# First normalization by token halves with renumbered weight slots, and another VectorE order in the feed-forward units

## The chip, the cores and the metric

One core of a Trainium2 chip runs the whole program. The metric is the device time of one execution in microseconds, lower is better. TensorE multiplies, VectorE, ScalarE and GpSimd work on tiles, and transfers go through queues, most of them SyncE's.

## What is computed

The reference is one layer for 512 tokens of width 1024 in float32: an adaptive modulation, a pooling branch and a recurrent branch mixed by gates, then

```python
mixed = (g_pool * y_pool + g_rwkv * y_rwkv) @ w_out[l]
x = layer_norm(ALPHA * x + (1 + gt1) * mixed, ln1_g[l], ln1_b[l], LN_EPS).astype(x.dtype)
h = x * (1 + sc2) + sh2
f = jnp.square(jax.nn.relu(h @ w_ff1[l])) @ w_ff2[l]
x = layer_norm(ALPHA * x + (1 + gt2) * f, ln2_g[l], ln2_b[l], LN_EPS).astype(x.dtype)
```

`w_out` is 1024x1024, `w_ff1` 1024x4096, `w_ff2` 4096x1024. The change concerns these five lines alone.

## The kernel before

**Split products.** Every float32 operand is split into a high part (ScalarE, `split_hi`, L762, or `split_again`, L1114) and a low part, raw minus high (GpSimd L669, L725 and L732, or VectorE `low_tile`, L1515). A product is three matmuls: high by high, low by high, high by low. Weights come in tiles of 128x1024 in order k; each tile has a slot of `w_hi` and `w_lo`, and its high part waits until TensorE is done with the tile that had the slot before.

**Output product** (L2184). The weights `w_out` are eight pairs o of 24 matmuls each. o=0 to 3 give columns 0 to 511, o=4 to 7 columns 512 to 1023, in four PSUM banks, one for each row block of 128 tokens. `take_out` (L1594, L1567) adds a bank to `xrows` and takes its statistics; `spreads` (L1574, L1575) and `columns` (L1580, L1581) make mean, variance and factors for two row blocks, ScalarE's `root` (L1067) the root between them.

**First normalization.** ScalarE normalizes row blocks 0 to 2 (L1072), VectorE block 3 (L1627). TensorE turns eight 128-column blocks f (L2191) into banks 4 to 7, 512 tokens each. For each f VectorE modulates (`h2_f32`, L1632), ScalarE makes the high part (L1081) and the residual `res` (L1082), and the low part is VectorE's for even f (L1635) and GpSimd's for odd f (L720). TensorE multiplies chunks 0 and 1 of `w_ff1` with each f as it comes (L2221), then chunks 2 and 3 (L2232). The high parts of the weights of chunks 2 and 3 stand in ScalarE's order behind its last residual, their low parts in GpSimd's order behind its last odd f. Chunks 0 and 1 use the slots of pairs o=6 and o=7.

**Units.** The feed-forward part runs in eight units of four chunks; units 1 to 6 are a hardware loop, unit 7 is written out. In a unit TensorE multiplies chunks 0 to 3 (48 + 24 + 24 matmuls of 512 columns), and ScalarE takes relu (L1089) and square (L1092) of each. The second product is a Winograd-like scheme: seven products of half-size blocks (`PRODUCTS`, 24 matmuls of 256 columns each, L2146) instead of eight. VectorE makes the sums of activations (`a_sums`, L1482 to L1486), their low parts (`low_raw` L1495, `low_sums` L1504), the sums of weights T1, T3, T2, T4 (L1528 to L1535), and adds each half product to `res` (`take`, L1563, two instructions). Product number at needs low part 4+at of the weights; those of numbers 3 to 6 are GpSimd's, in that order. A product waits until the one that had its PSUM banks before is taken: number 2 for number 0, 4 for 2, 5 for 3, 6 for 4. The second product needs `low_raw` of chunk 3 from its fourth matmul on. VectorE's order around chunk 3 is: low part of weight tile 6, T4, `lows` of chunk 3 (all three sums, `low_raw`, `low_sums`), then the fourteen takes.

**Tail.** In unit 7 TensorE turns `res` back in four steps (`turn_back`, L2124, order `BACK`), ScalarE copies the turned blocks to `xt2` (L1139), and VectorE takes statistics (L1688), makes the factors and applies them (`affine`, L1693, L1696) for row blocks 1, 2 and 3; ScalarE and GpSimd (L736, L737) do block 0. Each block is stored as it gets ready.

Of the kernel before, what the change touches and what calls it, by code (L numbers as in the profile page):

```python
# [6 lines left out]
P = 128  # L7
ALU = mybir.AluOpType
# [6 lines left out]
def build(nc, x, c, w_ada, b_ada, w_in, mu_shift, pool_mix, pool_scale, w_pool_up, w0, w_decay_up, a0,  # L15
# [6 lines left out]
    KT = D // P  # L22
# [23 lines left out]
    with ctx:  # L46
# [286 lines left out]
        SLOT = (2, 0, 1, 3, 2, 0, 1, 3, 2, 0, 1)  # L333
# [170 lines left out]
        BACK = ((0, 0, 2), (1, 1, 0), (0, 1, 2), (1, 0, 6))  # L504
# [30 lines left out]
        def _(sp):  # L535
# [79 lines left out]
        def _(pool):  # L615
# [101 lines left out]
            for f in range(1, KT, 2):  # L717
                pool.wait_ge(sem("h2_f32"), f + 1)
                pool.wait_ge(sem("h2_hi"), f + 1)
                link(pool.tensor_tensor(h2_lo[:, f, :], h2_f32(f), h2_hi[:, f, :].bitcast(F32), ALU.subtract), "h2_lo_by_pool")  # L720
# [19 lines left out]
        def _(act):  # L740
# [301 lines left out]
            for n in range(1, KT):  # L1042
# [14 lines left out]
                mixed_hi(n)  # L1057
            link(act.activation(small[:, 56:57], ones_col[:, :], ACT.Sqrt))
# [5 lines left out]
            def root(g, stage):  # L1064

                act.wait_ge(sem("ln_eps"), 2 * stage + g + 1)
                link(act.activation(small[:, 32 + 2 * g:34 + 2 * g], small[:, 28 + 2 * g:30 + 2 * g], ACT.Sqrt), "ln_std")  # L1067
# [5 lines left out]

            root(0, 0)
            normalise(0)
            normalise(1)
            root(1, 0)
            normalise(2)
            for f in range(KT):
                act.wait_ge(sem("h2_f32"), f + 1)  # L1080
                link(act.activation(h2_hi[:, f, :], h2_f32(f), ACT.Copy), "h2_hi")  # L1081
                link(act.activation(res[:, f, :], bank[4 + f % 4], ACT.Identity, scale=small[:, f:f + 1], bias=small[:, 8 + f:9 + f]), "res_ready")  # L1082
# [58 lines left out]
            for at in range(3):  # L1141
                out_tokens(at)
# [3 lines left out]
            out_tokens(3)  # L1146
# [3 lines left out]
        def _(dve):  # L1150
# [326 lines left out]
            def a_sums(link, n):  # L1477
# [5 lines left out]
                else:  # L1483
                    link(dve.tensor_tensor(a_sum[:, 1, :], x1, right(n)[:, S // 2:S], ALU.add))
                    link(dve.tensor_tensor(a_sum[:, 2, :], a_sum[:, 1, :], x0, ALU.subtract))
                    link(dve.tensor_tensor(a_sum[:, 3, :], right(n)[:, 0:S // 2], a_sum[:, 2, :], ALU.subtract), "a_summed")  # L1486
# [61 lines left out]
            def wait_half(unit, at, row, units=0):  # L1548
# [744 lines left out]
```

## Time and profile before

| | |
|---|---|
| Three runs | 1074.05, 1074.97 (median) and 1080.8 us |
| Profiled execution | 1072.6 us, span 1070.6 us |
| TensorE, VectorE, ScalarE, GpSimd busy | 91%, 64%, 44%, 34% of the span |
| One addition or statistics of 512 columns on VectorE | 0.69 us each |
| One aggregate on VectorE | 0.22 us |
| Normalization of 128 tokens on ScalarE | 1.25 us |
| Six passes of the unit loop | 738.1 to 999.1 us, 43.5 us each |

Times in the rows are microseconds from the start of the span. A timeline line gives start, duration (of all instructions of the line, if there are several), engine, line of the kernel, operation, output<-inputs, shapes and count; in brackets the engine's idle time before it and who ended it. In a line of the chain of waits stand start, length, engine, output, line and count.

### The profile page before, as it was taken

The page shows a single profiled execution, that of the slowest core. Times are in us where ns is not written, and L with a number is a line of the kernel's source. Part 1 is how long each engine was busy: PE and PEld are TensorE (multiplying, and loading weights), DVE is VectorE, ACT ScalarE, POOL GpSimd, SP SyncE. Part 2 cuts the span into 40 slices and gives each one's busy share as a digit, 9 for nine tenths or more (in the row PEclk, how much of TensorE's full clock was granted, in tenths as well). Part 3 has the DMA queues.
Part 4 walks back from the last instruction along what each step waited for, and adds up shares of the span by engine and source line. Part 5 has one row for each costly group of instructions (what it writes and reads, how often), then busy time and mean ns, then how long its engine had stood idle before and what let it go on. Part 6 is the DMA issues. An engine that isn't in the chain of part 4 may idle for free.

```text
span 1070.6 us, 27435 instructions
## 1 busy us (share of the span) xinstructions
PE 973.7 (91%) x11539; PEld 804.4 (75%) x11539; DVE 681.7 (64%) x940; ACT 468.9 (44%) x574; POOL 359.7 (34%) x218
## 2 busy tenths in 40 slices
PE   1798899999999999899999999699999999999993
PEld 1676677786777677577788888588889898898982
DVE  5735568578748858754221354657777777687778
ACT  0336445347335632436432251473544545445351
POOL 7332511411321132126444444235134052250431
PEclk9999999999999999999999999799999999999997
DMA  9332234224332424332543527114142251332101
GB/s 370 104 95 65 80 92 134 63 81 126 105 80 86 126 62 112 90 97 51 166 110 89 166 62 229 54 40 132 47 137 79 79 156 39 118 100 76 59 1 79
DMA packets 122918, 108.03 MB, mean 101 GB/s; under 512 B 5395, under 2 KB 104641, under 8 KB 122817
## 3 DMA queue, kind: packets, MB, share of 16 engines
q1 hardware_dynamic: 113009, 83.46, 26.1%
q10 hardware_dynamic: 9808, 23.08, 7.0%
q8 instruction: 81, 1.33, 0.5%
q14 instruction: 20, 0.16, 0.0%
HBM read 100.23 MB, written 2.10 MB: 96 GB/s over the span
## 4 chain that ended last, share of the span: by engine, by line
PE 68%; DVE 18%; ACT 5%; issue 3%; DMA 3%; POOL 2%; SPq 1%; ACTq 1%; DVEq 0%; POOLq 0%
PE bank L1787 11%; PE set L2146 10%; PE bank L2232 7%; PE set L2088 6%; PE bank L2088 5%; PE set L2232 4%; PE set L1841 4%; PE set L2184 3%; PE set L1853 2%; PE bank L2146 2%; PE set L1829 2%; PE bank L1768 2%; DVE Q L1234 1%; DVE w_lo L1515 1%; PE bank L2221 1%
## 5 line engine op out<-in xcount | busy, mean ns | idle before, releaser
L669 POOL TENSOR_TENSOR w_lo<-w_raw,w_hi 128x1024 fp32r<-128x1024 f32 (+2 forms) x75 | 171.0, 2280 | 380.7 <-ACT w_hi L762 380.3
L762 ACT ACTIVATE w_hi<-w_raw 128x1024 fp32r<-128x1024 f32 (+2 forms) x81 | 81.8, 1010 | 110.2 <-PE set L2088 36.1
L791 ACT ACTIVATE Q<-set 128x1024 f32<-128x1024 f32 x56 | 57.4, 1025 | 135.2 <-PE set L1841 69.0
L1787 PE MATMUL bank<-h_hi,w_hi 128*128 128x512 f32 x256 | 107.4, 419 | 3.5 <-POOL w_lo L669 3.3
L1563 DVE SCALAR_TENSOR_TENSOR res<-set,mod,res 128x256 f32<-128x256 f32 x192 | 92.9, 484 | 27.0 <-PE set L2146 19.0
L2146 PE MATMUL set<-a_hi,w_hi 128*128 128x256 f32 x384 | 108.6, 283 | 0.0
L2146 PE MATMUL set<-a_hi,w_lo 128*128 128x256 f32 x384 | 108.4, 282 | 0.0
L1114 ACT ACTIVATE w_hi<-w_raw 128x1024 fp32r<-128x1024 f32 x70 | 74.3, 1061 | 77.9 <-PE set L2146 69.9
L2146 PE MATMUL set<-a_lo,w_hi 128*128 128x256 f32 x384 | 108.3, 282 | 0.0
L1787 PE MATMUL bank<-h_hi,w_lo 128*128 128x512 f32 x256 | 102.4, 400 | 0.9 <-issue 0.9
L1787 PE MATMUL bank<-h_lo,w_hi 128*128 128x512 f32 x256 | 102.9, 402 | 0.0
L732 POOL TENSOR_TENSOR w_lo<-w_raw,w_hi 128x1024 fp32r<-128x1024 f32 x35 | 84.1, 2403 | 16.6 <-ACT w_hi L1114 13.3
L732 POOL TENSOR_TENSOR w_lo<-w_t,w_hi 128x1024 fp32r<-128x1024 f32 x7 | 16.8, 2405 | 189.0 <-ACT w_hi L1114 189.0
L2146 PEld LDWEIGHTS set<-a_lo,w_hi 128*128 128x128 f32 x384 | 73.0, 190 | 0.3
L2146 PEld LDWEIGHTS set<-a_hi,w_hi 128*128 128x128 f32 x384 | 72.9, 190 | 0.3
L2146 PEld LDWEIGHTS set<-a_hi,w_lo 128*128 128x128 f32 x384 | 72.9, 190 | 0.0
L1787 PEld LDWEIGHTS bank<-h_hi,w_hi 128*128 128x128 f32 x256 | 48.6, 190 | 20.2 <-issue 5.8
L1787 PEld LDWEIGHTS bank<-h_hi,w_lo 128*128 128x128 f32 x256 | 48.5, 189 | 11.2 <-issue 0.7
L1787 PEld LDWEIGHTS bank<-h_lo,w_hi 128*128 128x128 f32 x256 | 48.7, 190 | 9.5 <-issue 0.7
L1515 DVE TENSOR_TENSOR w_lo<-w_raw,w_hi 128x1024 fp32r<-128x1024 f32 x38 | 46.6, 1225 | 11.0 <-ACT w_hi L1114 7.5
L2232 PE MATMUL set<-h_hi,w_hi 128*128 128x512 f32 x128 | 50.6, 395 | 0.0
L2232 PE MATMUL set<-h_lo,w_hi 128*128 128x512 f32 x128 | 50.2, 392 | 0.0
(357 smaller groups left out, 2287.5 us busy)
## 6 DMA issues: line engine op xcount, KB each, us to landing
w_raw<-in_w_ff_dram SPq DMA_DIRECT2D x64, 512.0 KB, 4.0
w_raw<-in_w_in_dram SPq DMA_DIRECT2D x46, 512.0 KB, 3.9
y<-in_w_ada_dram ACTq DMA_DIRECT2D x20, 512.0 KB, 3.7
ada<-in_w_ada_dram SPq DMA_DIRECT2D x16, 512.0 KB, 9.4
Q<-in_w_ada_dram ACTq DMA_DIRECT2D x12, 512.0 KB, 4.1
w_raw<-in_w_rwkv_up_dram SPq DMA_DIRECT2D x8, 512.0 KB, 3.8
w_raw<-in_w_out_dram SPq DMA_DIRECT2D x8, 512.0 KB, 4.4
xtok<-in_x_dram SPq DMA_DIRECT2D x4, 512.0 KB, 9.6
```

The lines of the kernel that those rows point to most:

```text
L669: link(pool.tensor_tensor(part_of(k, w_lo), raw_part(k), part_of(k, w_hi).bitcast(F32), ALU.subtract), "lo_ready")
L732: again(pool.tensor_tensor(w_lo[SLOT[m]][:, :, :], raw[:, :, :], w_hi[SLOT[m]][:, :, :].bitcast(F32), ALU.subtract), "lo_ready")
L762: link(act.activation(part_of(k, w_hi), raw_part(k), ACT.Copy), "hi_ready")
L791: link(act.activation(by_half(tile), psum_flat(set_of(name)), ACT.Copy), "act_kept")
L1114: link(act.activation(w_hi[SLOT[m]][:, :, :], raw[:, :, :], ACT.Copy), "hi_ready")
L1515: link(dve.tensor_tensor(w_lo[slot][:, :, :], raw[:, :, :], w_hi[slot][:, :, :].bitcast(F32), ALU.subtract), "lo_by_dve")
L1563: link(dve.scalar_tensor_tensor(out=res[:, f, tokens], in0=product, scalar=mod[:, 40 + f:41 + f], in1=res[:, f, tokens], op0=ALU.mult, op1 ...
L1787: mm = pe.matmul(o, w, hx, start=(m == 0), stop=(m == 3 * KT - 1))
L1841: mm = pe.matmul(ps[N * p:N * p + N, q, c * C:(c + 1) * C], by_pair(left, p, q, c), by_pair(right, p, q, c), start=(m == 0), stop=(m == le ...
L2088: mm = pe.matmul(o, w[slot_of(k)][:, kt, :], hx[:, kt, :], start=(kt == 0 and m == 0), stop=(kt == kts - 1 and m == 2))
L2146: mm = pe.matmul(to, wx[:, i, columns], a[:, form, i, :], start=OPENS[at] and b == 0 and i == 0 and m == 0, stop=i == 1 and m == 2, skip_g ...
L2232: mm = pe.matmul(bank[m][:, :], w[slot][:, kt, :], hx[:, kt, :], start=(kt == 0 and at == 0), stop=(kt == KT - 1 and at == 2))
```

## The change

It does four things. (1) `SLOT` is renumbered: chunk 0's weights now follow pair o=5 in their slot, chunk 1's take a slot unused so far, chunks 2 and 3 follow o=6 and o=7. (2) The last two pairs of the output product run for row blocks 0 and 1 first, and the first normalization, its transposes, modulation, high and low parts, residuals and the products of chunks 0 and 1 run for tokens 0 to 255 first (g=0), then for 256 to 511 (g=1). VectorE normalizes blocks 1 and 3, ScalarE blocks 0 and 2; LN_EPS is added as the bias of ScalarE's root. ScalarE's high parts for chunks 2 and 3 still follow its last residual. (3) In every unit VectorE's order around chunk 3 is `last_lows`, with the first product's takes between and T4 behind. (4) In unit 7 the fifth and sixth product are swapped, and the tail is in another order: statistics and gains of row blocks 2 and 3 read PSUM, block 1 is finished last.

```diff
-        SLOT = (2, 0, 1, 3, 2, 0, 1, 3, 2, 0, 1)
+        SLOT = (1, 3, 2, 0, 1, 3, 2, 0, 1, 3, 2)
...
+        TURN = ((4, 4, 5, 5, 2, 2, 3, 3), (6, 6, 7, 7, 4, 4, 5, 5))
...
-        BACK = ((0, 0, 2), (1, 1, 0), (0, 1, 2), (1, 0, 6))
+        BACK = ((0, 0, 2), (0, 1, 0), (1, 1, 2), (1, 0, 6))
+        PLAIN, LAST = (0, 1, 2, 3, 4, 5, 6), (0, 1, 2, 3, 5, 4, 6)
...
-            for j in (1, 0, 2, 3):
+            for j in (0, 2, 3, 1):
...
+            for g in range(2):
+                for f in range(1, KT, 2):
+                    pool.wait_ge(sem("h2_f32"), g * KT + f + 1)
+                    pool.wait_ge(sem("h2_hi"), g * KT + f + 1)
+                    link(pool.tensor_tensor(h2_lo[:, f, side(g)], h2_f32(f)[:, side(g)], h2_hi[:, f, side(g)].bitcast(F32), ALU.subtract), "h2_lo_by_pool")
...
             root(0, 0)
             normalise(0)
-            normalise(1)
+            for f in range(2):
+                row_high(0, f)
             root(1, 0)
+            for f in range(2, 4):
+                row_high(0, f)
             normalise(2)
+            for f in range(4, KT):
+                row_high(0, f)
+            for f in range(4):
+                residual(0, f)
+            for f in range(4):
+                row_high(1, f)
+            for f in range(4, KT):
+                residual(0, f)
+            for f in range(4, KT):
+                row_high(1, f)
             for f in range(KT):
...
+                residual(1, f)
             for m in range(2, 4):
                 split_hi(K_FF + m)
...
+            def last_lows(link, n, unit, units=0):
+
+                a_sums(link, n, 0)
+                low_raw(link, n, units)
+                a_sums(link, n, 1)
+                take(link, unit, 0, 0, units)
+                low_sums(link, n, units)
+                take(link, unit, 0, 1, units)
+                summed(link, "T4", unit, units)
...
             take_out(0, 1)
             take_out(1, 1)
             spreads(0)
             take_out(2, 1)
             columns(0, 0)
+            x_hat(1)
+            modulated(0, 0)
+            modulated(0, 1)
             take_out(3, 1)
+            row_low(0, 0)
             spreads(1)
+            modulated(0, 2)
+            modulated(0, 3)
             columns(1, 0)
...
+            x_hat(3)
+            row_low(0, 2)
+            for g, f in ((0, 4), (0, 6), (1, 0), (1, 2), (1, 4), (1, 6)):
+                modulated(g, f)
+                modulated(g, f + 1)
+                row_low(g, f)
...
                 if m == 2:
                     low_tile(link, 6, 0)
-                    summed(link, "T4", 0)
...
+            for at in LAST[1:5]:
                 for row in range(2):
...
+                    last_take(at, row)
+            turned_statistics(0)
+            last_take(LAST[5], 0)
             turned_statistics(1)
...
+            last_take(LAST[5], 1)
+            spreads(0)
+            last_take(LAST[6], 0)
+            columns(0, 1)
+            last_take(LAST[6], 1)
             turned_statistics(2)
...
             turned_statistics(3)
             spreads(1)
...
+            dve.wait_ge(sem("rows_in"), 32)
+            gain(2)
+            dve.wait_ge(sem("ln_std"), 4)
+            link(dve.reciprocal(small[:, 38:40], small[:, 34:36]))
+            shift(2)
+            gain(3)
+            shift(3)
+            gain(1)
+            shift(1)
...
+            for g in range(2):
+                for o in (NOUT - 2, NOUT - 1):
...
+                    mm = out_rows(o, (2 * g, 2 * g + 1))
...
+            for g in range(2):
+                for kt in range(KT):
+                    pe.wait_ge(sem(("h2_lo_by_dve", "h2_lo_by_pool")[kt % 2]), g * (KT // 2) + kt // 2 + 1)
...
+                    if g == 0 and kt == 5:
+                        pe.wait_ge(sem("out_taken"), 2 * TB)
+                        pe.wait_ge(sem("x_hat_by_dve"), 2)
+                        pe.wait_ge(sem("x_hat"), 2)
+                        for f in range(4):
+                            turn(1, f)
+                    if g == 0 and kt == KT - 1:
+                        for f in range(4, KT):
+                            pe.wait_ge(sem("res_ready"), (2, 4)[f // 6])
+                            turn(1, f)
...
             for m in (2, 3):
+                pe.wait_ge(sem("res_ready"), (6, 8)[m - 2])
                 hidden_chunk(m, 0, 0)
```

`row_high`, `residual`, `modulated` and `row_low` are the instructions of L1081, L1082, L1632 and L1635 on 256 tokens. `gain` is the first half of `affine` (for blocks 2 and 3 two instructions that read 512 columns from PSUM), `shift` the second.

## Rows read from the trace of the kernel before

**Rows 1.** The page's chain that ended last, by engine.

```profile
PE 68%; DVE 18%; ACT 5%; issue 3%; DMA 3%; POOL 2%; SPq 1%; ACTq 1%; DVEq 0%; POOLq 0%
```

**Rows 2.** Timeline of TensorE: turn, a unit, the last matmul.

```profile
686.49 1.09 PE L2191 MATMUL set<-ident,xrows 128*128 128x128 f32 x4 [6.42 <-ACT xrows L1072]
...
724.87 0.47 PE L2146 MATMUL bank<-a_hi,w_hi 128*128 128x256 f32 x1 [2.72 <-DVE a_lo L1495]
...
900.60 0.39 PE L2146 MATMUL bank<-a_hi,w_hi 128*128 128x256 f32 x1 [1.00 <-DVE a_lo L1495]
...
1050.72 0.28 PE L2146 MATMUL set<-a_hi,w_lo 128*128 128x256 f32 x1
```

**Rows 3.** Busy time by stretch: stretch, length, engines, granted clock, DMA share, GB/s.

```profile
681.00:724.90 43.90, 33.88 (x156) 28.10 (x156) 28.75 (x42) 30.38 (x43) 12.29 (x7) 0.84 0.16 45
...
686.50:690.00 3.50, 2.65 (x12) 2.25 (x13) 1.69 (x4) 1.32 (x2) 0.00 (x0) 0.50 0.19 58
```

**Rows 4.** Chain of waits in a unit: matmuls of 512, then of 256 columns.

```profile
885.28 5.62 PE set L2232 x24
...
903.39 10.65 PE set L2146 x89
```

**Rows 5.** Timeline of VectorE: the last instruction.

```profile
1066.25 1.28 DVE L1696 SCALAR_TENSOR_TENSOR xt<-xt,small,ln_rows 128x1024 f32<-128x1024 f32 x1
```

**Rows 6.** Timeline of GpSimd: low parts before and in the turn.

```profile
653.69 2.40 POOL L669 TENSOR_TENSOR w_lo<-w_raw,w_hi 128x1024 fp32r<-128x1024 f32 x1 [3.19 <-ACT w_hi L762]
...
681.38 2.34 POOL L669 TENSOR_TENSOR w_lo<-w_raw,w_hi 128x1024 fp32r<-128x1024 f32 x1 [3.19 <-ACT w_hi L762]
```

**Rows 7.** Timeline of VectorE before and in the turn.

```profile
655.07 2.10 DVE L1543 TENSOR_TENSOR w_raw<-w_raw,gate 128x1024 f32<-128x1024 f32 x1 [3.22 <-DMA w_raw<-in_w_out_dram]
...
671.05 1.22 DVE L1528 TENSOR_TENSOR w_t<-w_raw 128x1024 f32<-128x1024 f32 x1 [8.06 <-DMA w_raw<-in_w_ff_dram]
...
681.78 1.96 DVE L1581 SCALAR_TENSOR_TENSOR small<-small 128x2 f32<-128x2 f32 x1
...
689.45 1.66 DVE L1632 TENSOR_SCALAR t<-set,mod 128x512 f32<-128x512 f32 x2 [1.56 <-PE set L2191]
```

**Rows 8.** Timeline early in the kernel: VectorE one, then two operations; GpSimd.

```profile
112.92 0.69 DVE L1309 TENSOR_TENSOR Q<-t 128x512 f32<-128x512 f32 x1
113.65 3.00 DVE L1441 TENSOR_TENSOR Q<-G 128x512 f32<-128x512 f32 x2
...
113.76 2.34 POOL L701 TENSOR_TENSOR Q<-Q,DC 128x1024 f32<-128x1024 f32 x1 [3.14 <-DVE Q L1309]
```

**Rows 9.** Timeline of ScalarE at the end of the turn.

```profile
701.88 0.63 ACT L1081 ACTIVATE h_hi<-left 128x512 fp32r<-128x512 f32 x1 [0.38 <-DVE left L1632]
702.54 0.78 ACT L1082 ACTIVATE res<-set,small 128x512 f32<-128x512 f32 x1
703.35 2.15 ACT L762 ACTIVATE w_hi<-w_raw 128x1024 fp32r<-128x1024 f32 x2
...
708.53 0.42 ACT L1011 ACTIVATE a_hi<-left 128x256 fp32r<-128x256 f32 x1
```

**Rows 10.** Timeline of VectorE around chunk 3 of a unit.

```profile
897.12 1.23 DVE L1535 TENSOR_TENSOR w_raw<-w_raw 128x1024 f32<-128x1024 f32 x1
898.38 0.43 DVE L1484 TENSOR_TENSOR a_sum<-left,right_odd 128x256 f32<-128x256 f32 x1
...
899.85 0.69 DVE L1495 TENSOR_TENSOR a_lo<-right_odd,a_hi 128x512 fp32r<-128x512 f32 x1
900.70 0.96 DVE L1504 TENSOR_TENSOR a_lo<-a_sum,a_hi 128x768 fp32r<-128x768 f32 x1 [0.15 <-ACT a_hi L1022]
...
906.12 4.30 DVE L1563 SCALAR_TENSOR_TENSOR res<-set,mod,res 128x256 f32<-128x256 f32 x8
```

**Rows 11.** Timeline of ScalarE: the square of chunk 3.

```profile
897.11 0.63 ACT L1092 ACTIVATE right_odd<-t 128x512 f32<-128x512 f32 x1
```

**Rows 12.** Timeline of GpSimd: first of a unit's four low parts for products.

```profile
901.84 2.41 POOL L732 TENSOR_TENSOR w_lo<-w_t,w_hi 128x1024 fp32r<-128x1024 f32 x1 [26.94 <-ACT w_hi L1114]
```

More of the change, by code:

```diff
@@ L1699, in _, with gain @@
-            for at in range(NFORM - 1):
+                    if half == 0:
+                        dve.wait_ge(sem("out_tokens"), 2 * at + row + 1)
+                    else:
+                        dve.wait_ge(sem("turned_back"), at + 1)
+                    link(dve.bn_stats(stat[:, 2 * j + z, :], bank[first + row] if half else xt2[:, j, z * S:(z + 1) * S]))
+            def gain(j):
+                mean = small[:, 20 + 2 * j:21 + 2 * j]
+                if j < 2:
+                    link(dve.scalar_tensor_tensor(out=xt2[:, j, :], in0=xt2[:, j, :], scalar=mean, in1=ln_rows[:, 0, :],
+                                                  op0=ALU.subtract, op1=ALU.mult))
+                    return
+                for half, z, first in BACK[2:]:
+                    columns_of = slice(z * S, (z + 1) * S)
+                    link(dve.scalar_tensor_tensor(out=xt2[:, j, columns_of], in0=bank[first + j % 2], scalar=mean, in1=ln_rows[:, 0, columns_of],
+                                                  op0=ALU.subtract, op1=ALU.mult))
@@ L2136, in quarters @@
                         free(at, row)
[L2137 to L2138 removed]
+                        if at in (2, 4, 5, 6):
+                            freed = sequence.index(FREED_BY[at])
+                            pe.wait_ge(sem("taken"), units * (2 * NFORM) + (2 * NFORM * unit + 2 * freed + row + 1))
                         for b in range(2):
@@ L2149, in quarters @@
                             mm.then_inc(sem("half_made"), 1)
-                            if last and at == NFORM - 1:
+                            if last and place == 5:
+                                taken_through(unit, 4, units)
+                                turn_back(1)
+                            if last and place == 6:
                                 taken_through(unit, 5, units)
@@ L2154, in quarters @@
                     mm.then_inc(sem("w_used"), 1)
-                    if last and at == 3:
+                    if last and place == 3:
                         taken_through(unit, 1, units)
                         turn_back(0)
-                    if last and at == 5:
-                        taken_through(unit, 4, units)
-                        turn_back(1)
                 if last:
@@ L2170, in _, with out_rows @@
                 pool_up(n)
-            for o in range(NOUT):
+            def out_rows(o, rows):
+                z, at = o // 4, o % 4
+                wh, wl = two_by(w_hi[slot_of(K_OUT + o)]), two_by(w_lo[slot_of(K_OUT + o)])
+                for j in rows:
+                    for i in range(2):
+                        for m, (a, w) in enumerate(((mix_hi, wh), (mix_lo, wh), (mix_hi, wl))):
+                            mm = pe.matmul(bank[OUT_BANKS[z][j]], a[:, 2 * at + i, j * P:(j + 1) * P], w[:, i, :],
+                                           start=at == 0 and i == 0 and m == 0, stop=at == 3 and i == 1 and m == 2)
+                    if at == 3 and j < TB - 1:
+                        mm.then_inc(sem("out_made"), 1)
+                return mm
+            for o in range(NOUT - 2):
                 z, at = o // 4, o % 4
```

189 lines of the change are left out of this document (84 added, 105 removed).

## Prediction

> **What bounds the kernel now.** I read the chain of waits first: 68% of the span is on TensorE, 18% on VectorE, 5% on ScalarE [rows 1]. The change touches three stretches, so each is read by itself in the timelines.
>
> *The turn from attention to feed-forward* (669 to 743 us): the last two weight pairs of the output product, the first normalization, and unit 0. TensorE waits 6.42 us before the first transpose and 2.72 us before the fourth matmul of unit 0's second product [rows 2]. After the first wait it is granted 0.50 of its clock, 1.2 GHz, so that a matmul takes twice as long [rows 3]; at 2.4 GHz 24 matmuls of 512 columns take 5.62 us [rows 4].
>
> *The units* (43.5 us each): TensorE rests only once, 1.00 us idle (1.16 us of issue, as these matmuls stand 0.12 apart), for VectorE's low part of chunk 3 [rows 2, 4].
>
> *The tail*: from the last matmul (1050.72 + 0.28) VectorE carries the chain to 1067.5 [rows 2, 5].
>
> **Turn, step 1: renumbered slots.** Chunk 0 now follows pair o=5 in its slot, chunk 1 an unused slot. Chunk 1's high part waits today for o=7, so that its low part runs on GpSimd at 681.38, and VectorE's multiply of two columns, begun at 681.78, takes 1.96 us, until that is over [rows 6, 7]. Pair o=5 ends 48 matmuls of 0.234 us before 680.1, at 668.9. So both high parts (1.06 us) run from 669.2 and GpSimd's two low parts from 670.3. The 1.96 us goes.
> It comes back elsewhere. VectorE's weight sums T1 and T3 start at 671.05, when their weights land, 1.22 us each [rows 7]. GpSimd is idle there now, and won't be. What that means a row shows: a multiply of two SBUF tiles, begun at 655.07 inside GpSimd's 653.69 to 656.09, took 2.10 us, to 1.08 us past GpSimd's end [rows 6, 7]. And two such 512-column operations, usually 0.69 us, took 3.00 us together with a GpSimd operation that began 0.11 us after them: the engines alternate [rows 8]. So T1 ends at 672.7 + 1.08 = 673.7, GpSimd's second part is held and ends at 676.0, and T3 ends at 677.1, not 673.5.
>
> **Turn, step 2: token halves.** Tokens 0 to 255 of o=6 and o=7 are multiplied first and are there at 674.7; VectorE comes to them at 677.1. Three additions and three statistics (0.69 and a gap, by the table), two aggregates (0.25) and two small columns (0.2) bring it to 682.4. ScalarE normalizes 128 tokens in 1.25 us, and transposes start at 683.7, 2.8 us earlier than now.
> From here an operation on 512 tokens becomes two on 256. ScalarE copies 512 columns in 0.63 us and 256 in 0.42; its residual from PSUM (0.78 us for 512) isn't shown for 256: I take 0.78 - 0.21 = 0.57, bounds 0.42 and 0.78 [rows 9]. So ScalarE's 8 x 0.66 + 8 x 0.81 = 11.8 us become 16 x 0.45 + 16 x 0.60 = 16.8. VectorE's modulation (1.66 us for two, [rows 7]) becomes 0.54, bounds 0.43 and 0.83. I step the queues with these prices. VectorE modulates from 684.3, takes the last addition and statistics in between, and gives the second half's spread at 687.8; ScalarE has the high parts of columns 0 to 3 and its row 2 done at 690.7. From 691.7 it works almost without a break: 12 high parts (5.4), 16 residuals (9.4) and some 2.7 us of short waits for VectorE, so its last residual ends at 709.2, where it now ends at 703.3 [rows 9]. TensorE has chunks 0 and 1 done at 706.2 (now 707.5), behind VectorE's last low part at 704.6 and GpSimd's at 705.3.
> Behind those residuals in ScalarE's order stand the high parts of chunks 2 and 3, now at 703.35 [rows 9]. After the change: high part done at 710.3, GpSimd's low part 2.4 us later, chunk 2 at 712.8 instead of 707.7. TensorE has then waited 6.6 us, as long as the 6.42 that led to 0.50 of the clock [rows 2, 3], so I charge 5.4 us of chunk 2 at half speed, 2.7 us lost (bounds 1.7 and 5). Chunk 3 ends at 712.8 + 11.2 + 2.7 = 726.8, now 718.8: +8.0.
> Against that, the low parts of chunks 0 and 1 are long done: the 2.72 us wait shrinks to about 0.2, and the half-speed stretch behind it (3.4 us, 1.7 lost) goes: -4.2. T4's new place adds 0.9, next part. The turn: +8.0 - 4.2 + 0.9 = +4.7 us (bounds +2.5 and +9).
>
> **Units: T4 moved.** For chunk 3 VectorE now does T4 (1.23 us), three sums (0.46 each), the low part (0.69), the low sums (0.96), then the takes [rows 10]. T4 moves behind the first product's takes, the low part in front of the third sum. ScalarE's square of chunk 3 ends at 897.74 [rows 11]; 0.15 + 0.92 + 0.12 + 0.69 later, at 899.6, the low part is done, not at 900.54. Of 1.16 us 0.2 stays: -0.95.
> At T4's old place GpSimd was idle. At the new one it isn't: it runs four low parts end to end from 901.84, 2.41 us each [rows 12]. New order: third sum to 900.1, take (1.0) to 901.1, low sums to 902.1, take to 903.2, then T4. GpSimd starts at 902.1 and holds to 904.5, so T4 ends at 905.6, not 904.45. Three takes of 1.08 (eight instructions, two to a take, come to 4.30 [rows 10]) end at 908.85. The third frees the bank of the fifth product, which TensorE reaches at 899.64 + 2.62 + 2 x 2.88 = 908.0 (24 matmuls of 0.12, [rows 4]). It stands there 0.85 us, about 0.2 more with the hand-overs: -0.95 + 1.05 = +0.1 a unit, +0.6 over the loop's six. Bounds: -6 if T4 isn't held, +3 if it is held through a second low part in some units.
> The Trainium skill (SBUF — State Buffer, Who interferes with whom) states the rule: a VectorE instruction with two SBUF inputs contends with a GpSimd instruction that reads SBUF, the loser fully blocks, and one with at most one SBUF input doesn't contend. The trace agrees with both halves, the takes (one input in PSUM) among them. It speaks against the change: by it the units gain nothing, without it some 0.9 us each.
>
> **Tail.** The last unit's held matmul (today at 1031.3) comes 0.95 earlier, its fourth product ends at 1030.3 + 2.62 + 5.76 = 1038.7, the first turn back at 1039.5. The sixth product, now fifth in turn, needs the fourth's bank. VectorE ends T4 6 us after the held matmul, at 1036.3, and takes four row halves before this one, so the bank is free at 1041.7. TensorE waits 2.2 us, and from there its products and turn backs (0.8 each), with one more wait of 1.05 for a take behind statistics, end at 1053.3; VectorE's last take at 1054.65. Then four statistics, two aggregates, two gains from PSUM (0.78 a half, bounds 0.69 and 0.96), a reciprocal, three shifts and one gain at 1.32 [rows 5]: 2.8 + 0.45 + 3.1 + 0.2 + 5.3 = 11.9, so 1066.6, 0.9 us before now. The 2.2 us wait lies near the 2.72 us one, after which the clock fell, so I charge 1.8 us at half speed: +0.9 (bounds -1.5 and +3). The last store is a whole row block as now.
>
> **Sum.** +4.7 + 0.6 + 0.9 = +6.2 us. The profiled execution took 1072.6 us for a span of 1070.6 and would take 1078.8. The median shown, 1074.97, lies 2.4 above it; on that scale the forecast is 1081.2.
>
> **Rivals.**
> *T4 isn't held* (not slower than before): VectorE streams its second input beside GpSimd. For it: the eight take instructions run beside GpSimd at 0.54 us each [rows 10, 12]. Against: the 2.10 us row. It decides where T4 ends: by 904.5 the bank is free in time. Of the forecast go 0.6 + 6.0 in the loop, 0.9 in unit 0 and 1.8 in the tail: 1081.2 - 9.3 = 1071.9.
> *The halves pay* (faster): ScalarE keeps up, chunk 2's weights are ready at 706.2, chunk 3 ends at 717.4, 1.4 early. The turn is -1.4 - 4.2 + 0.9 = -4.7: 1081.2 - 9.4 = 1071.8. For it: ScalarE is busy only 30.4 of 43.9 us there [rows 3]. Against: its order puts eight second-half residuals ahead of the weights. Both together: 1062.5.
> *TensorE stays cold* (slower still): the gaps between halves keep 0.50 until chunk 2 and beyond: turn +9, units +0.2 each, tail +1.5, in all +11.7: 1086.7.
>
> **How the numbers follow.** Forecast 0.55, T4 free 0.13, halves pay 0.12, both 0.04, cold 0.16. A measurement tells about 1% (10.7 us) from no change. Faster by over 1% (under 1064.2) is the joint case and its fringe, 0.06; slower by over 1% (over 1085.7) most of the cold case and a little of the forecast, 0.16; within, 0.78. The range of 8 in 10 takes in both single rivals and the start of the cold case: 1070 to 1086.5.
>
> **What would show it.** T3 ending near 677 and a first transpose near 683.7; a TensorE wait of over 5 us before chunk 2, released by GpSimd, and 0.50 of the clock behind it; T4 at about 2.4 us in each unit, no wait at the second product but 0.9 us at the fifth, period 43.6. It is wrong if T4 takes 1.23 us beside GpSimd, if the period is under 43.0, or if chunk 2 starts right behind chunks 0 and 1.

## The result, and the profile after

| | before | after |
|---|---|---|
| median, same chip | 1079.46 us (14 runs) | 1084.47 us (14 runs) |
| ratio, 95% interval | | 1.0054 [1.0029, 1.0079] |
| profiled execution, its span | 1072.6, 1070.6 us | 1076.59, 1074.8 us |

The change makes the kernel half a per cent slower. The forecast was a ratio of 1.0058 (1081.2 us on the scale of the median shown first). The share of each stage, in us, from the two profiled executions; "product end" is the last matmul of the output product, a unit begins with its first hidden matmul:

| stage | before | after | forecast |
|---|---|---|---|
| turn: product end to unit 1 | 63.2 | 68.1 | +4.7 |
| the loop's six units | 261.2 (43.50 each, the first 43.73) | 261.6 (43.59) | +0.6 |
| last unit to VectorE's last instruction | 63.0 | 61.7 | +0.9 |

So +4.9, +0.35 and -1.3: +3.9 us. The span grew by 4.2; the rest, 0.27 us, lies ahead of the turn.

Timeline of TensorE after, in the turn, a unit and the tail; it answers to [rows 2]:

```profile
684.17 3.60 PE L2285 MATMUL set<-ident,xrows 128*128 128x128 f32 x16 [3.83 <-ACT xrows L1085]
...
713.97 0.77 PE L2325 MATMUL set<-h_hi,w_hi 128*128 128x512 f32 x1 [5.37 <-POOL w_lo L679]
...
739.77 0.36 PE L2228 MATMUL set<-a_hi,w_hi 128*128 128x256 f32 x1 [0.79 <-issue]
...
914.13 0.38 PE L2228 MATMUL set<-a_hi,w_hi 128*128 128x256 f32 x1 [0.95 <-DVE res L1606]
...
1046.77 0.36 PE L2228 MATMUL set<-a_hi,w_hi 128*128 128x256 f32 x1 [1.94 <-POOL w_lo L743]
```

The first transpose comes 3.83 us after the product instead of 6.42. Then TensorE stands 5.37 us before chunk 2, for a low part of GpSimd. In the units the 1.00 us wait at the second product is replaced by 0.95 at the fifth, now for a take. (The last row names a low part as releaser; what ended that wait is read off further down.) Unit 0 has a wait of 0.79 us at the same place; it ends 0.10 us after a take that runs from 738.66 to 739.67. Busy time by stretch, columns as in [rows 3]:

```profile
684.20:688.00 3.80, 3.57 (x16) 3.17 (x16) 2.54 (x5) 0.83 (x2) 0.72 (x1) 0.55 0.00 0
688.00:704.10 16.10, 12.13 (x90) 10.98 (x91) 11.65 (x25) 11.06 (x22) 4.30 (x6) 1.00 0.01 2
704.10:708.60 4.50, 4.50 (x24) 4.25 (x23) 1.25 (x3) 3.76 (x8) 1.25 (x2) 0.62 0.00 0
708.60:714.00 5.40, 0.03 (x2) 0.06 (x1) 0.18 (x1) 5.17 (x8) 2.44 (x2) 0.77 0.00 0
714.00:718.00 4.00, 4.00 (x10) 3.17 (x11) 3.90 (x4) 3.28 (x6) 2.48 (x1) 0.50 0.52 142
```

Behind the first wait the clock is at 0.55 for a short stretch only, but it drops twice again: 0.62 on average while chunks 0 and 1 end, and 0.50 in the four microseconds from 714. While TensorE waits before chunk 2, ScalarE is busy 5.17 of 5.40 us. Its timeline shows with what (answers to [rows 9]):

```profile
695.43 2.36 ACT L1093 ACTIVATE res<-set,small 128x256 f32<-128x256 f32 x4
697.82 0.87 ACT L1089 ACTIVATE h_hi<-t 128x256 fp32r<-128x256 f32 x2
...
705.51 4.75 ACT L1093 ACTIVATE res<-set,small 128x256 f32<-128x256 f32 x8
710.28 2.14 ACT L773 ACTIVATE w_hi<-w_raw 128x1024 fp32r<-128x1024 f32 x2
```

Residuals of 256 columns, 0.59 us each, stand in front of the high parts of chunks 2 and 3. VectorE and GpSimd at T1 and T3 and in a unit (answers to [rows 7], [rows 6], [rows 10] and [rows 12]):

```profile
671.29 2.80 DVE L1571 TENSOR_TENSOR w_t<-w_raw 128x1024 f32<-128x1024 f32 x1 [8.04 <-DMA w_raw<-in_w_ff_dram]
674.12 3.32 DVE L1574 TENSOR_TENSOR w_raw<-w_raw 128x1024 f32<-128x1024 f32 x1
...
947.53 0.69 DVE L1528 TENSOR_TENSOR a_lo<-right_odd,a_hi 128x512 fp32r<-128x512 f32 x1
...
951.97 2.33 DVE L1578 TENSOR_TENSOR w_raw<-w_raw 128x1024 f32<-128x1024 f32 x1
954.42 2.04 DVE L1606 SCALAR_TENSOR_TENSOR res<-bank,mod,res 128x256 f32<-128x256 f32 x4
```

```profile
670.60 5.76 POOL L679 TENSOR_TENSOR w_lo<-w_raw,w_hi 128x1024 fp32r<-128x1024 f32 x2 [3.19 <-ACT w_hi L773]
...
711.48 5.00 POOL L679 TENSOR_TENSOR w_lo<-w_raw,w_hi 128x1024 fp32r<-128x1024 f32 x2 [5.11 <-ACT w_hi L773]
...
950.79 2.42 POOL L743 TENSOR_TENSOR w_lo<-w_t,w_hi 128x1024 fp32r<-128x1024 f32 x1 [27.09 <-ACT w_hi L1146]
953.37 3.19 POOL L743 TENSOR_TENSOR w_lo<-w_raw,w_hi 128x1024 fp32r<-128x1024 f32 x1 [0.16 <-POOL w_lo L743]
```

T4 (951.97) begins inside a low part, ends 1.09 us after that one's end at 953.21, and the next low part takes 3.19 instead of 2.4 us: it in turn ends 2.26 us after T4. This is what "held" means in this text. The takes run beside these low parts at their usual 0.5 us a piece.

### The profile page after: what moved, and what is told of

It reads as the page before. It is cut to its first block, busy times and chain, and to the rows that moved or that the text cites. A ratio compares the mean times of both kernels' runs of the same rounds, so it can differ in the third digit from the quotient of the medians.

```text
span 1074.8 us, 27588 instructions
## 1 busy us (share of the span) xinstructions
PE 975.2 (91%) x11587; PEld 806.2 (75%) x11587; DVE 697.6 (65%) x950; ACT 470.2 (44%) x586; POOL 369.5 (34%) x222
## 4 chain that ended last, share of the span: by engine, by line
PE 45%; issue 21%; DVE 14%; POOL 12%; ACT 3%; DMA 2%; SPq 0%; POOLq 0%; ACTq 0%; DVEq 0%
PE bank L1866 12%; POOL w_lo L743 10%; PE set L2167 6%; PE bank L2167 5%; PE set L1920 4%; PE set L2259 3%; PE set L1932 2%; PE set L1908 2%; PE bank L1847 2%; PE set L2325 1%; PE set L1944 1%; DVE Q L1265 1%; DMA ptab<-in_mu_shift_dram 1%; PE bank L2259 1%; POOL w_lo L679 1%
## 5 line engine op out<-in xcount | busy, mean ns | idle before, releaser
L743 POOL TENSOR_TENSOR w_lo<-w_raw,w_hi 128x1024 fp32r<-128x1024 f32 x35 | 89.4, 2553 | 9.2 <-ACT w_hi L1146 5.8
L1866 PEld LDWEIGHTS bank<-h_hi,w_hi 128*128 128x128 f32 x256 | 48.6, 190 | 21.2 <-issue 6.8
L1866 PEld LDWEIGHTS bank<-h_hi,w_lo 128*128 128x128 f32 x256 | 48.6, 190 | 11.2 <-issue 0.7
L2325 PE MATMUL set<-h_hi,w_lo 128*128 128x512 f32 x128 | 50.9, 397 | 0.0
```

The costliest lines, as they stand in the source:

```text
L743: again(pool.tensor_tensor(w_lo[SLOT[m]][:, :, :], raw[:, :, :], w_hi[SLOT[m]][:, :, :].bitcast(F32), ALU.subtract), "lo_ready")
L1866: mm = pe.matmul(o, w, hx, start=(m == 0), stop=(m == 3 * KT - 1))
L2325: mm = pe.matmul(bank[m][:, :], w[slot][:, kt, :], hx[:, kt, :], start=(kt == 0 and at == 0), stop=(kt == KT - 1 and at == 2))
```

## The experiments

The theory after the result: the halves put 16 short residuals on ScalarE ahead of chunk 2's weights (the 5.37 us), and T4's new place takes back what VectorE's new order gives. The product ended anywhere from 680.1 to 695.8 us in the profiled executions of what follows, with a granted clock lower in other slices before it, as the page's clock row shows for after and then for f2 (the turn lies in the 26th to 28th slice):

```profile
PEclk9999999999999999999999999989999999999997
```

```profile
PEclk9698998999989999979999999989999999999997
```

So the runs are compared by stages, and by the ratio where it was timed. The stages of a run come from its one profiled execution.

| run | turn | unit | tail | ratio to before |
|---|---|---|---|---|
| before | 63.2 | 43.50 | 63.0 | |
| after | 68.1 | 43.59 | 61.7 | 1.0054 [1.0029, 1.0079] |
| e1 old VectorE order in after | 69.4 | 43.26 | 60.4 | 1.0012 [0.9972, 1.0052] |
| e2 chunk 2 and 3 high parts first | 65.0 | 43.60 | 61.7 | 1.0003 [0.9975, 1.0031] |
| e3 T4 back, rest of the order new | 69.1 | 42.80 | 60.9 | 0.998 [0.9941, 1.002] |
| e4 four short low parts | 67.0 | 42.50 | 60.4 | profiled only |
| f1 before, slots alone | 62.7 | 43.36 | 62.8 | 0.9996 [0.9964, 1.0028] |
| f3 after without the halves | 58.7 | 43.59 | 61.7 | 0.995 [0.9914, 0.9986] |
| f2 before, order and tail new, T4 in front | 62.3 | 42.93 | 61.4 | 0.995 [0.9915, 0.9984] |
| f4 = f2 with the new slots | 60.8 | 42.80 | 61.3 | 0.993 [0.9897, 0.9963] |
| g1 = f4, T4 late in unit 0 | 59.0 | 42.80 | 61.3 | 0.9926 [0.9899, 0.9954] |
| g2 = g1, first wait filled | 58.3 | 42.79 | 61.3 | 0.9899 [0.987, 0.9927] |
| g3 after, wait of chunk 2 filled | 66.4 | 43.59 | 61.7 | 1.0052 [1.0027, 1.0078] |

How far one execution can be trusted for the turn can be read from after, e1, e3 and e4. Up to chunk 2 they run the same code. Chunk 2 starts 33.6, 34.4, 34.5 and 33.3 us after the product, behind waits of 5.37, 6.57, 6.56 and 6.55 us, and chunks 2 and 3 take 13.2, 14.0, 14.0 and 13.5 us, as the half clock there lasts 4.4, 6.0, 6.2 and 5.0 us. A difference of a turn under some 1.5 us is therefore not shown by the table alone. In after the clock is back at 1.00 from 718.4, 4.4 us behind chunk 2's start; e3 is still at 0.50 5 us behind it:

```profile
724.00 0.77 PE L2326 MATMUL set<-h_hi,w_hi 128*128 128x512 f32 x1 [6.56 <-POOL w_lo L679]
```

```profile
728.70:729.55 0.85, 0.85 (x3) 0.66 (x3) 0.70 (x2) 0.45 (x2) 0.00 (x0) 0.50 1.14 343
```

### VectorE's order and T4's place

```
-                a_sums(link, n, 0)
-                low_raw(link, n, units)
-                a_sums(link, n, 1)
-                take(link, unit, 0, 0, units)
-                low_sums(link, n, units)
-                take(link, unit, 0, 1, units)
-                summed(link, "T4", unit, units)
+                lows(link, n, units)
+                take(link, unit, 0, 0, units)
+                take(link, unit, 0, 1, units)
...
+                if m == 3:
+                    summed(link, "T4", 0)
```

> The changed kernel with VectorE's old order around chunk 3 in all units (T4, three sums, low part, low sums, then the takes). Theory (T4 is held by GpSimd, so the new order gives back what it gains): T4 takes 1.23 us again instead of 2.3 to 2.5, the wait at the second product is back at 1.0 us and the one of 0.95 us at the fifth goes, the unit period falls only from 43.59 to 43.50. In the last unit the bank of the fourth product is free 2 us earlier and the weight's low part 1 us earlier, so the wait of 1.94 us at the fifth place goes and the tail ends about 1.5 us earlier. In all some 2.5 us faster than the changed kernel (1072 of span in a run whose clock is as in the profile shown), ratio to before about 1.003. Rival (T4 isn't held, the new order is a gain of 0.9 us a unit): period 44.5, in all 6 us slower than the changed kernel.

Measured: 43.26 us a unit where 43.50 was expected, the wait back at the second product (0.81 us, where before has 1.00), the tail 1.3 us shorter than in after. That T4 isn't held in its new place, which called for 44.5, is out. For the next run T4 alone is moved back to its place after chunk 2's low tile:

```
                 take(link, unit, 0, 1, units)
-                summed(link, "T4", unit, units)
...
                 if m == 2:
                     low_tile(link, 6, 0)
+                    summed(link, "T4", 0)
```

> The changed kernel with T4 back in front of chunk 3's sums, everything else of the new order kept (low part before the third sum, takes of the first product between). VectorE waits 0.7 us there in the changed kernel, so T4 (1.23 us, GpSimd idle) costs only about 0.5 us of delay. Theory (the hold of T4 is the whole price of the new order): no wait at the fifth product, a wait of 0.5 us at the second, period 43.1 instead of 43.59, unit 0 0.5 us shorter, and the tail's wait at the fifth place falls from 1.94 to under 0.5. In all 4 to 5 us faster than the changed kernel, ratio to before about 1.001. Rival (the takes between the sums are what delays the fifth product): period stays at 43.5 or more.

Measured: T4 1.23 us, a single wait of 0.35 us, 42.80 us a unit, more than the theory promised. In the tail the wait is 0.68 us instead of 1.94. The turn isn't shorter (69.1), for the clock reason above: from the first product of unit 0 to unit 1 it takes 20.6 us where after takes 21.2. The order without T4's move is worth 0.8 us a unit against after. The last of the three keeps T4 late and cuts GpSimd's four low parts for products 3 to 6 to 8 of their columns, so the low parts of those weights are left out otherwise:

```
-                    again(pool.tensor_tensor(w_lo[SLOT[m]][:, :, :], raw[:, :, :], w_hi[SLOT[m]][:, :, :].bitcast(F32), ALU.subtract), "lo_ready")
+                    n = P if m < 4 else 1
+                    again(pool.tensor_tensor(w_lo[SLOT[m]][:, :, 0:n], raw[:, :, 0:n], w_hi[SLOT[m]][:, :, 0:n].bitcast(F32), ALU.subtract), "lo_ready")
```

> The changed kernel in which GpSimd makes the low parts of the four weight tiles for the last four products of each unit for 8 of 1024 columns only (the other columns' low parts are left out, so the output isn't the reference's). The waits and the order stay. Theory (T4 is held by GpSimd's long operation and by nothing else): T4 takes 1.23 us in every unit, no wait at the fifth product, period 42.6 to 42.7, the tail's wait at the fifth place under 1 us. Rival (T4 is slow in its new place for another reason, such as transfers into the weight tiles): T4 stays at 2.3 us or more and the period at 43.6.

Timeline of VectorE in this run, the T4 of one unit, and of GpSimd beside it:

```profile
907.00 1.22 DVE L1579 TENSOR_TENSOR w_raw<-w_raw 128x1024 f32<-128x1024 f32 x1
```

```profile
906.91 0.22 POOL L744 TENSOR_TENSOR w_lo<-w_raw,w_hi 128x8 fp32r<-128x8 f32 x1 [0.88 <-ACT w_hi L1147]
```

T4 stands in its late place and takes 1.22 us, TensorE no longer waits in a unit, and the unit takes 42.50. So it is the low parts beside it that hold T4, not its place in the order, and that hold is what costs the units their gain: 0.8 us each by e3, 1.1 by this run, in which GpSimd is also free sooner.

### What stands before chunk 2

```
+            for m in range(2, 4):
+                split_hi(K_FF + m)
             for f in range(KT):
                 residual(1, f)
-            for m in range(2, 4):
-                split_hi(K_FF + m)
```

> The changed kernel with ScalarE's high parts of chunks 2 and 3 in front of the eight residuals of the second token half. Theory (ScalarE's order delays the weights): these high parts end at 707.6, GpSimd's first low part at about 709.1, chunk 2 starts there instead of 713.97, the wait of 5.4 us before it falls to about 2.0 and the half-speed stretch behind it goes. Residuals end 2.1 us later, at 712.4, where relu of chunk 0 starts as now, so the chain over ScalarE and VectorE through the four chunks becomes the limit: TensorE waits some 3 to 4 us at the fourth matmul of the second product, and unit 1 starts 1.5 to 2.5 us earlier than 748.4 rather than 5. Rival (VectorE's first-half values, not ScalarE's order, are the limit): chunk 2 starts at 713.5 to 714 as now.

```profile
712.47 0.77 PE L2325 MATMUL set<-h_hi,w_hi 128*128 128x512 f32 x1 [1.81 <-POOL w_lo L679]
...
730.96 0.38 PE L2228 MATMUL bank<-a_hi,w_hi 128*128 128x256 f32 x1 [2.43 <-DVE a_lo L1528]
```

The wait before chunk 2 falls from 5.37 to 1.81 us, as the theory had it: ScalarE's order made it. But a new wait of 2.43 us comes at the second product, and of 5.1 us (28.5 instead of 33.6 after the product, for chunk 2's start) 3.1 are left in the turn. The next run takes the halves out altogether; GpSimd, ScalarE, VectorE and TensorE have the turn of the kernel before, everything else stays new:

```
-            for g in range(2):
-                for o in (NOUT - 2, NOUT - 1):
...
+            for o in range(NOUT):
...
-            for f in range(KT):
-                residual(1, f)
...
+                link(act.activation(h2_hi[:, f, :], h2_f32(f), ACT.Copy), "h2_hi")
+                link(act.activation(res[:, f, :], bank[4 + f % 4], ACT.Identity, scale=small[:, f:f + 1], bias=small[:, 8 + f:9 + f]), "res_ready")
```

> The changed kernel with the first normalization of the kernel before (all 512 tokens at once), its new slots, unit order and tail kept. Theory (the token halves are what costs, because 16 residuals on ScalarE stand ahead of chunk 2's high part): no wait of 5 us before chunk 2, turn about 60 + 0.9 = 61 us where the changed kernel has 68.1, period 43.6, tail 61.7: some 7 us below the changed kernel, ratio to the kernel before 0.997. Rival (the halves cost little, and the 5 us come from VectorE's new order in unit 0): the turn stays at 66 us or more, ratio 1.003 or more.

```profile
691.96 1.09 PE L2236 MATMUL set<-ident,xrows 128*128 128x128 f32 x4 [5.09 <-ACT xrows L1084]
...
727.61 0.38 PE L2191 MATMUL bank<-a_hi,w_hi 128*128 128x256 f32 x1 [1.07 <-DVE a_lo L1508]
```

The first transpose is 1.3 us later than with the halves (5.09 instead of 3.83 after the product), the turn 9.4 us shorter, 2.3 more than the theory had. The halves cost more than the whole change does. Of the 9.4, 8.4 are there at chunk 2's start (25.2 us after the product instead of 33.6). The order of ScalarE's queue accounts for 5.1 of these (e2); how the other 3.3 divide over the engines no run shows.

### The slots alone

```
-        SLOT = (2, 0, 1, 3, 2, 0, 1, 3, 2, 0, 1)
+        SLOT = (1, 3, 2, 0, 1, 3, 2, 0, 1, 3, 2)
```

> The kernel before with the renumbered slots alone. Theory 1 (the renumbering is the part of the change that pays in the turn, since the low parts of chunks 0 and 1 are made 6 us sooner): GpSimd runs two low parts back to back from 670.3, T1 and T3 are held to 2.8 and 3.3 us, the 1.96 us multiply is back at 0.2 us, the 2.72 us wait in unit 0's second product and the half clock behind it go, so the stretch from the end of the output product to unit 1 shrinks from 63.2 to about 60 us. If the period of 43.26 us seen in the run with the order undone comes from the slots too, the units show 43.26 instead of 43.50, 1.4 us over the loop. Together about 4.5 us less than before, ratio 0.996. Rival (slots move nothing that TensorE waits for): the turn stays at 63.2 within 0.5, the period at 43.50, ratio 1.000.

```profile
677.15 2.88 DVE L1528 TENSOR_TENSOR w_t<-w_raw 128x1024 f32<-128x1024 f32 x1 [7.95 <-DMA w_raw<-in_w_ff_dram]
680.07 3.31 DVE L1531 TENSOR_TENSOR w_raw<-w_raw 128x1024 f32<-128x1024 f32 x1
...
688.66 0.16 DVE L1581 SCALAR_TENSOR_TENSOR small<-small 128x2 f32<-128x2 f32 x1
```

```profile
691.58 1.09 PE L2191 MATMUL set<-ident,xrows 128*128 128x128 f32 x4 [5.30 <-ACT xrows L1072]
...
729.30 0.58 PE L2146 MATMUL bank<-a_hi,w_hi 128*128 128x256 f32 x1 [2.75 <-DVE a_lo L1495]
```

The low parts do come sooner, T1 and T3 are held, the two-column multiply is back at 0.16 us, and the first wait is 1.1 us shorter. But the second wait stays: 2.75 us, as 2.72 in [rows 2]. The theory is wrong there: that wait is for VectorE's low part of chunk 3, and chunks 0 and 1 have no part in it. Together the slots move nothing that the medians show.

In the stages they do move something. The first product starts 36.9 us after the output product instead of 38.7. But in f1 the half clock behind the second wait lasts 6.8 us (728.6 to 735.4) where before has 3.4 (725.1 to 728.5), and this takes most of it back. Between f2 and f4, below, where both have 3.4 us there, the first wait falls from 6.42 to 5.10 us and the turn by 1.5 us.

### The parts that pay

Order and tail of the change, but T4 in front, on the kernel before; then with the slots:

```
+                take(link, unit, 0, 0, units)
+                low_sums(link, n, units)
+                take(link, unit, 0, 1, units)
...
                     summed(link, "T4", 1, units)
```

> The kernel before with VectorE's low part of chunk 3 ahead of the third sum and the first takes between, T4 left where it was, and the new tail; slots and first normalization as before. Theory (T4's place beside GpSimd's low parts is all that takes the new order's gain): T4 1.23 us, TensorE waits 0.35 us in a unit instead of 1.00, period 42.8 instead of 43.5, 4.2 us over the loop, tail 60.9 instead of 63.0; together -6.3 us, ratio 0.994. Rival (the shorter period came from the new slots): period 43.1 or more, ratio 0.997 or more.

> The same as the run before it, with the renumbered slots as well. If the gains of the slots (turn 3 us) and of the order (6.3 us) add up: turn about 60 us, period 42.8 us, tail 60.9 us, some 9 us less than before, ratio 0.991. If the earlier weights bring nothing without the halves: as the run before it, ratio 0.994.

Measured: 42.93 and 42.80 us a unit, tails 61.4 and 61.3, turn 60.8 (f4). The rival, 43.1 or more a unit with the old slots, is out. In unit 0 TensorE still waits 2.29 us (f4) where f3, with T4 late, waits 1.07; hence the next run:

```
                 take(link, unit, 0, 1, units)
+                if unit == 0:
+                    summed(link, "T4", unit, units)
```

> The run with order and slots together (f4), but T4 behind the first product's takes in unit 0 only, where GpSimd makes fewer low parts; in the loop and the last unit T4 stays in front. Theory (T4 ahead of chunk 3 delays that chunk's low part in unit 0, so that TensorE waits 2.3 us and is then at half clock for 3.4): turn 58.7 us as in the run with only the turn undone, instead of 60.9, period 42.8, tail 61.3; ratio to the kernel before 0.991. Rival (the turns of 58.7 and 60.9 differ by chance, through where the clock fell): turn 60.9, ratio 0.993.

Turn 59.0 instead of 60.8 us, as expected. The ratio, 0.9926, can't be told from f4's 0.993, but both are below both kernels, as their intervals show.

### The price of the half clock

The prediction charged half clock in three places. Two runs take it away by giving TensorE matmuls that no output needs, where it waits:

```
             pe.wait_ge(sem("out_taken"), TB)
+            for m in range(20):
+                pe.matmul(bank[0][:, :], mix_hi[:, 0, 0:P], mix_hi[:, m % KT, :], start=True, stop=True)
```

> The same, with 20 matmuls of 512 columns more (4.7 us) into a bank that is overwritten afterwards, between the output product and the first transpose: they change no output and fill the wait of 5.1 us. Theory (the wait is what takes the clock to 1.2 GHz): the granted clock stays at 1.00 through the transposes and chunks 0 and 1, the first transpose starts as before the edit, the 10.3 us at half clock go and with them about 5 us: turn 54 us, ratio 0.986. Rival (the transposes and the loosely filled start of chunks 0 and 1 take it down as well): some half clock remains behind them, gain 0 to 2 us, ratio 0.990.

Busy time by stretch of g1, from the product's end on, then of g2:

```profile
685.30:695.30 10.00, 3.91 (x16) 3.14 (x16) 6.87 (x16) 5.24 (x7) 0.00 (x0) 0.73 0.00 1
695.30:710.70 15.40, 14.78 (x64) 12.24 (x65) 7.45 (x10) 12.85 (x18) 8.12 (x6) 0.84 0.01 2
```

```profile
694.70:704.70 10.00, 6.83 (x37) 5.21 (x35) 7.21 (x17) 5.48 (x7) 0.00 (x0) 1.00 0.00 1
704.70:718.90 14.20, 13.26 (x64) 10.43 (x64) 7.21 (x10) 13.32 (x19) 7.56 (x5) 1.00 0.01 2
```

The clock stays at 1.00 through the whole turn; in g1 some 10 us were at half. Yet the turn shrinks by 0.7 us, less than executions of one code can differ, and not by 5:

```profile
701.94 1.53 PE L2238 MATMUL set<-ident,xrows 128*128 128x128 f32 x12 [1.47 <-ACT xrows L1084]
705.09 0.63 PE L2238 MATMUL set<-ident,xrows 128*128 128x128 f32 x4 [1.62 <-DVE h_lo L1658]
...
718.96 0.50 PE L2281 MATMUL set<-h_hi,w_hi 128*128 128x512 f32 x1 [0.58 <-POOL w_lo L679]
...
735.12 0.39 PE L2193 MATMUL bank<-a_hi,w_hi 128*128 128x256 f32 x1 [1.59 <-DVE a_lo L1508]
```

A faster TensorE meets longer waits: 1.47 and 1.62 us where g1 has 0.95 and 0.68, a new 0.58, and 1.59 for 1.07. By chunk 2's start 1.3 us are gained (24.2 us after the product instead of 25.5), and 0.5 of them go again at the second product. ScalarE is busy 13.32 of 14.20 us in the second stretch: it has next to nothing to give there, and TensorE's half clock lay mostly hidden beside it. That ScalarE alone is the bound is a reading of the busy times; no run made it faster. Each theory of this run was half right: the clock is fully there, as the first had it, and nearly nothing is gained, which only the second allowed. The ratio of 0.9899 is the lowest of all, its interval overlapping with g1's.

```
                 pe.wait_ge(sem("res_ready"), (6, 8)[m - 2])
+                if m == 2:
+                    for n in range(22):
+                        pe.matmul(bank[2][:, :], h2_hi[:, 0, 0:P], h2_hi[:, n % KT, :], start=True, stop=True)
```

> The changed kernel with 22 matmuls of 512 columns more (5.1 us) into chunk 2's bank before chunk 2, in its wait of 5.37 us: they change no output. Theory (the prediction's term for chunk 2: the wait for ScalarE's residuals and GpSimd's low part costs what it shows, and the half clock behind it 3.4 us more): chunk 2 starts at the same time after the output product, the 6.8 us at half clock behind the wait go, turn 68.1 - 3.4 = 64.7 us, ratio to the kernel before 1.002. Rival (the clock falls because of the loose matmuls of chunks 0 and 1 before the wait): the half clock stays and the added matmuls delay chunk 2, ratio 1.006 or more.

```profile
713.20:719.90 6.70, 5.21 (x25) 3.98 (x23) 0.10 (x1) 6.38 (x11) 2.37 (x1) 1.00 0.00 0
719.90:731.10 11.20, 11.20 (x48) 9.10 (x49) 10.35 (x14) 7.82 (x13) 2.58 (x1) 1.00 0.35 95
```

Chunk 2 starts 33.4 us after the product (after: 33.6), at full clock, and chunks 2 and 3 take 11.2 us where after takes 13.2: 2.0 us for the half clock. Of these 0.5 come back as a wait of 0.50 us at the second product, so the turn gains 1.7 with the 0.25 at chunk 2's start. The theory had 3.4 and a ratio of 1.002; the ratio measured, 1.0052, shows no gain. Against e1 and e3, whose chunks 2 and 3 take 14.0 us, the half clock there is worth 2.8 us.

## Why the prediction was right, and where it was not

**The sum.** The ratio forecast, 1.0058, lies almost on the measured 1.0054, and that is in part luck. The stages of the two profiled executions add up to +3.9 us where +6.2 stood, and these two executions are 1.0037 apart; the medians differ by 5.0 us; the interval reaches from 1.0029 to 1.0079. The turn, the largest term, came by the mechanism forecast. The tail was off by 2.2 us and had the wrong sign.

**Slots, step 1: right.** T3 was to end at 677.1; it ended at 677.44. The 1.96 us multiply went, and f1 shows both with the slots alone. The rule of the Trainium skill (SBUF — State Buffer, Who interferes with whom) agrees with the trace in both halves again: T1, T3 and T4 are held, the takes with one input in PSUM are not. (T1 2.80 us, T3 3.32, T4 2.33, where 1.22 is usual; the takes 0.51.)

**Halves, step 2: right, size and mechanism.** First transpose forecast at 683.7, found at 684.17; the 256-column residual 0.57, found 0.59; last residual 709.2 against 710.26; chunk 2 at 712.8 against 713.97, released by GpSimd as said. e2 and f3 show that the halves and ScalarE's queue make that wait. Of the 1.2 us between, 1.1 are there at the last residual, and 0.27 of these are the later product; the rest I did not trace. TensorE was to end chunks 0 and 1 at 706.2 and ended them at 708.6, after 3.4 us at half clock from 704.7 that the prediction didn't have; hence 5.37 us of wait and not 6.6. In e1, e3 and e4, where the clock stays up there, the wait is 6.6 us as forecast. (The prediction's end of chunk 3, 726.8, is 726.7 by its own terms, and 16 residuals at 0.60 us are 9.6 us, not 9.4.)

**Half clock behind that wait: right where the wait is 6.6 us.** Charged 2.7 us. g3 shows that it cost 2.0 in after's profiled execution, and 1.7 in the turn; by the same measure, chunks 2 and 3 against g3's 11.2 us, e1 and e3 lost 2.8, e4 2.3. In after the smaller loss hid 0.7 of the 1.2 us above: the first product started 46.9 us after the output product's end instead of 38.7, +8.2 where +8.0 stood.

**The 2.72 us wait: right number, wrong reason.** The prediction let it shrink "since the low parts of chunks 0 and 1 are long done". f1 has them done and still waits 2.75 us. It shrinks with VectorE's order: to 2.29 us with T4 in front (f4), to 1.07 with T4 late (f3, g1). With the halves and an earlier chunk 2 it is 2.43 (e2), and with chunk 2 at its late place and the old order it is 0.79 (e1). Only the late chunk 2 and the new order together leave nothing of it in after. The row names the low part of a right half, a_lo, as releaser [rows 2]: I should have followed that to VectorE's order and not to the weights. The half clock behind it lasted 3.4 us in before, as the prediction took it; two rows of before from there:

```profile
725.12:725.97 0.85, 0.85 (x5) 0.85 (x5) 0.84 (x1) 0.85 (x1) 0.00 (x0) 0.50 0.79 306
...
727.67:728.52 0.85, 0.85 (x7) 0.85 (x6) 0.81 (x2) 0.00 (x0) 0.85 (x1) 0.55 0.00 0
```

T4's new place was to add 0.9 us in unit 0: it adds the 0.79 us wait at the fifth product, which e1, e3 and e4 don't have. From the first product to unit 1 the turn went from 24.5 to 21.2 us, -3.3, which is the -4.2 + 0.9 of the forecast.

**Units: right.** T4 2.33 us (2.31 to 2.56 over the units) where 2.4 stood, 0.95 us at the fifth product where 0.85 and 0.2 stood, +0.09 us each where +0.1 stood. The loop as a whole grew by 0.35 and not 0.6, as the first unit of before takes 43.73 us. e3 and e4 rule out the rival that T4 isn't held: without low parts beside it T4 takes 1.22 us and the units gain 1.0 against before, which is what that rival had.

**Tail: the term that was mis-sized.** Forecast +0.9, found -1.3. The wait before the sixth product came, 1.94 us for 2.2, and for the bank, as forecast, although the row names a low part as releaser. These are VectorE's takes and GpSimd's low part of that product:

```profile
1043.59 4.12 DVE L1606 SCALAR_TENSOR_TENSOR res<-set,mod,res 128x256 f32<-128x256 f32 x8
```

```profile
1043.89 2.35 POOL L743 TENSOR_TENSOR w_lo<-w_raw,w_hi 128x1024 fp32r<-128x1024 f32 x1 [0.16 <-POOL w_lo L743]
```

The low part is over at 1046.24. The take that frees the bank is the third of these four, two instructions each, and ends at 1046.67; TensorE goes on at 1046.77, 0.10 later, as it does behind the takes in the units (957.72 behind 957.59) and in unit 0. In e3, with T4 in front, the wait is 0.68 us, and there it does end with the low part, 0.05 us after it. The 1.8 us of half clock charged behind the wait did not come, as the busy time by stretch shows for after:

```profile
1046.70:1048.70 2.00, 1.93 (x16) 1.96 (x17) 1.12 (x3) 0.00 (x0) 2.00 (x1) 1.00 0.03 8
```

The clock stays at 1.00 up to 1063, behind the last product. Without that charge the step gives -0.9. The rest, 0.4, is there by VectorE's last take: 49.7 us after the unit's start, where 1054.65 - 1004.5 = 50.1 stood. The charge rested on the likeness of 2.2 us to the 2.72 us wait, and no row showed a wait in between.

**The rivals.** The halves do not pay: f3 says the opposite, 9.4 us. TensorE doesn't stay cold: 1.00 from 688 to 704.1. What a colder start of the turn costs, e1 and e3 show: before the end of chunk 1 they are at half clock for 13.6 us, after for twice 3.4, and they start chunk 2 only 0.8 us later than after.

Open: a unit takes 43.36 us with the new slots alone (f1) and 43.26 with slots and tail in after's program (e1), not 43.50. The wait in it falls from 1.00 to 0.92 and 0.81; no run says what a slot's number has to do with it.

## What to carry to other kernels

Splitting a serial step in halves starts it earlier but doubles the instructions of every engine behind it; add up the busiest of them first, with what is queued behind it. Here the halves cost 9.4 us for a transpose 1.3 us sooner, and 5.1 us of chunk 2's delay came from two high parts queued behind ScalarE's last eight residuals. When an edit is a bundle, run its parts: the order with T4 left in place, the new slots and the new tail together are at 0.993 of the kernel before, and the whole change at 1.0054. And where two things are waited for, compare the times at which each ended with the start of the waiting instruction before believing the releaser that a row names.

## What the hardware did that was not expected

- TensorE's half clock costs only where TensorE is the bound: 10 us at half clock ahead of chunk 2 were worth 0.7 us in the turn (g1, g2), while 4.4 us behind chunk 2's wait cost 2.0 (after against g3) and 6.0 and 6.2 us there 2.8 (e1, e3).
- In or behind TensorE's unfilled waits of 3.83 us and more in the turn the clock fell, in every run; 20 added matmuls of 512 columns in the wait kept it at 1.00, even through the waits of 1.47 and 1.62 us that follow. The tail's wait of 1.94 us was not followed by half clock either, while the one of 2.72 us in before was, and f4's of 2.29 us, here with the stretch behind it. The length of a single wait doesn't decide it: after's wait of 1.50 us before 703.86 was followed by half clock from 704.7, e4's of 1.49 us at the same place in the same code was not.

```profile
728.00:730.50 2.50, 2.50 (x13) 2.50 (x13) 2.36 (x5) 2.44 (x3) 0.69 (x1) 0.50 0.23 87
```

- The hold between VectorE and GpSimd works both ways and in turns: T4 waited for the low part at 950.79 to end, then the next low part waited for T4, and took 3.19 us. Such a chain, set by no wait of the program, delays both things that the tail's sixth product needs: its bank (1046.67) and its low part (1046.24).
